# Cross-attention keys and queries: rounded weights meet both halves of x in one 512-column matmul

## The reference, cut to what matters

```
def memory_cross_attention(h, mem_n, w_q, w_kv, w_o):
    q = (h @ w_q).reshape(B, S, 4, 256)                    # "xq": queries
    kv = (mem_n @ w_kv).reshape(B, 256, 2, 4, 256)         # "K": keys, "V": values
    k, v = kv[:, :, 0], kv[:, :, 1]
    s = einsum('bthd,bmhd->bhtm', q, k) * 256 ** -0.5
    p = softmax(s, axis=-1)
    return einsum('bhtm,bmhd->bthd', p, v).reshape(B, S, 1024) @ w_o
```

## Time and profile before

| | us |
|---|---|
| median of 3 runs | 1287.78 (1287.45 to 1287.88) |
| the profiled execution's own time | 1287.96 |
| its span in the trace | 1286.2 |
| PE busy | 1273.2 (99%) |
| PEld busy | 1105.7 (86%) |
| DVE busy | 891.3 (69%) |
| ACT busy | 695.1 (54%) |
| DMA, mean share of its 16 engines for the weight queue | 51.6% |

### The profile page before, as it was taken

The page is one execution under the profiler, slowest core; times in us unless marked ns, Lnnn a source line. Parts: engine busy times, 40 slices in busy tenths (PEclk is TensorE's granted clock), DMA queues, the critical chain, the costliest instruction groups (busy, mean ns, idle before and its releaser), DMA issues.

```text
span 1286.2 us, 17766 instructions
## 1 busy us (share of the span) xinstructions
PE 1273.2 (99%) x7337; PEld 1105.7 (86%) x7337; DVE 891.3 (69%) x1053; ACT 695.1 (54%) x976; POOL 115.0 (9%) x176
## 2 busy tenths in 40 slices
PE   7999999999999999999999999999999999999999
PEld 7889898988888988889888888898887888888887
DVE  4657775776666776877676666767885566887775
ACT  5755554644444656565554444565565654655443
POOL 6200100100000100020100000101330003100000
PEclk9999999999999999999999999999999999999999
DMA  8754644556555543354455565563544445465552
GB/s 267 262 164 144 201 163 131 183 195 196 196 188 183 186 164 127 137 177 151 153 177 195 196 196 191 169 197 99 164 164 139 157 134 194 139 214 184 186 195 98
DMA packets 156113, 223.64 MB, mean 174 GB/s; under 512 B 6103, under 2 KB 107635, under 8 KB 156032
## 3 DMA queue, kind: packets, MB, share of 16 engines
q1 hardware_dynamic: 154528, 219.23, 51.6%
q0 software_dynamic: 1376, 3.22, 0.7%
q10 hardware_dynamic: 128, 0.05, 0.0%
HBM read 221.44 MB, written 1.05 MB: 173 GB/s over the span
## 4 chain that ended last, share of the span: by engine, by line
PE 90%; DVE 5%; ACT 2%; issue 1%; DMA 1%; POOL 0%; SPq 0%; ACTq 0%; DVEq 0%
PE ps L443 18%; PE ps L496 9%; PE ps L445 9%; PE ps L498 9%; PE ps L497 9%; PE ps L426 5%; PE ps L428 5%; PE ps L427 5%; PE ps L678 5%; PE ps L680 5%; PE ps L679 5%; DVE wlo L1803 2%; PE ps L517 1%; ACT whi L1221 1%; PE ps L461 1%
## 5 line engine op out<-in xcount | busy, mean ns | idle before, releaser
L1221 ACT ACTIVATE whi<-raw 128x1024 fp32r<-128x1024 f32 x411 | 424.5, 1052 | 313.8 <-PE ps L443 154.8
L1803 DVE TENSOR_TENSOR wlo<-raw,whi 128x1024 fp32r<-128x1024 f32 x408 | 490.1, 1232 | 140.4 <-ACT whi L1221 137.8
L443 PE MATMUL ps<-RR,whi 128*128 128x512 f32 x1024 | 353.9, 396 | 0.4 <-DVE wlo L1803 0.4
L445 PE MATMUL ps<-RR,wlo 128*128 128x256 f32 x1024 | 264.8, 279 | 0.1
L496 PE MATMUL ps<-whi,RR 128*128 128x512 f32 x592 | 236.7, 400 | 0.7 <-DVE wlo L1803 0.5
L498 PE MATMUL ps<-whi,RR 128*128 128x512 f32 x592 | 231.0, 390 | 0.0
L497 PE MATMUL ps<-wlo,RR 128*128 128x512 f32 x592 | 230.9, 390 | 0.0
L443 PEld LDWEIGHTS ps<-RR,whi 128*128 128x128 f32 x1024 | 184.9, 188 | 36.1 <-issue 0.7
L445 PEld LDWEIGHTS ps<-RR,wlo 128*128 128x128 f32 x1024 | 193.0, 188 | 11.9 <-DVE RR L1834 0.4
L426 PE MATMUL ps<-RR,whi 128*128 128x256 f32 x512 | 147.1, 287 | 0.9 <-DVE RR L1834 0.8
L428 PE MATMUL ps<-RR,wlo 128*128 128x256 f32 x512 | 144.8, 283 | 0.0
(11 more groups left out here) (357 smaller groups left out, 1311.9 us busy)
## 6 DMA issues: line engine op xcount, KB each, us to landing
raw<-in_ffn_w_gate_up SPq DMA_DIRECT2D x44, 1024.0 KB, 5.1
raw<-in_ffn_w_down SPq DMA_DIRECT2D x33, 1024.0 KB, 4.9
raw<-in_w_in SPq DMA_DIRECT2D x28, 1024.0 KB, 5.0
raw<-in_ffn_w_up SPq DMA_DIRECT2D x22, 1024.0 KB, 5.1
raw<-in_xa_w_kv SPq DMA_DIRECT2D x16, 1024.0 KB, 5.2
raw<-in_sb_w_qkv SPq DMA_DIRECT2D x12, 1024.0 KB, 5.1
raw<-in_ml_w_in SPq DMA_DIRECT2D x11, 1024.0 KB, 6.9
raw<-in_xa_w_q SPq DMA_DIRECT2D x8, 1024.0 KB, 5.2
```

The source lines that it names most:

```text
L443: m = pe.matmul(two(ps[:, bank, :]), p.hi[:, k, :], XT2[:, k, :, :], start=k == 0, stop=k == 7)
L445: pe.matmul(ps[:, bank, 0:256], p.lo[:, k, :], X.h[:, k, :], start=False, stop=False)
L1221: act.activation(p.hi, p.raw, ACT.Copy).then_inc(S["w_hi"], 2 if p.n == pool_piece.n + 1 else 1)
L1803: dve.tensor_tensor(p.lo, p.raw, p.hi.bitcast(F32), ALU.subtract).then_inc(S["w_lo"], 2 if p.n in (2, late_piece.n + 1) else 1)
```

## The change

For K0_0 to K0_3, K1_0 to K1_2 and all eight query chunks, `fm_piece` gives way to a new function `fm_wide`: eight matmuls of whi with hi and lo of x side by side (512 columns), then eight of wlo with hi of x (256 columns). The piece waits for `w_hi` before the first eight and for `w_lo` only before the second eight. Each piece now fills a whole bank, so a chunk takes two banks, and both halves of each must be added. ACT still copies only the first half of the banks (the rounded copy now rounds the first half). DVE does two instructions where it did one: lo = first half - hi, then, after the end of that, lo = lo + second half. For K0_1, whose banks are 0 and 3, both steps are done bank by bank, in four instructions of 256 columns. The banks are dealt out anew, with two new waits of TensorE on `K_dve` (before K0_2 and before K1_2), and its wait for `ml_og` 4 now stands ahead of K0_1. K1_3 stays narrow.

```diff
+            def fm_wide(name, X, banks, i):
+
+                p, o = C[name].pieces[i], ps[:, banks[i], :]
+                pe.wait_ge(S["w_hi"], p.n + 1)
+                for k in range(8):
+                    if X.met <= k:
+                        pe.wait_ge(X.sem, X.need[k])
+                        X.met = k + 1
+                    pe.matmul(two(o), p.hi[:, k, :], X.both[:, k, :, :], start=k == 0, stop=False)
+                pe.wait_ge(S["w_lo"], p.n + 1)
+                for k in range(8):
+                    m = pe.matmul(o[:, 0:256], p.lo[:, k, :], X.h[:, k, :], start=False, stop=k == 7)
+                m.then_inc(S["w_used"], 1)
...
             def keys(l, j, bank, M):
-                fm(f"K{l}_{j}", M, bank)
+                for i in range(2):
+                    fm_wide(f"K{l}_{j}", M, bank, i)
...
-            keys(0, 0, 1, M)
+            keys(0, 0, (1, 2), M)
...
-            keys(0, 1, 2, M)
             pe.wait_ge(S["ml_og"], 4)
-            keys(0, 2, 3, M)
+            keys(0, 1, (0, 3), M)
+            pe.wait_ge(S["K_dve"], 1)
+            keys(0, 2, (1, 2), M)
...
-            keys(1, 0, 4, M)
-            keys(1, 1, 5, M)
+            keys(1, 0, (6, 7), M)
+            keys(1, 1, (4, 5), M)
             X = norm_rows(2)
-            keys(1, 2, 6, M)
+            pe.wait_ge(S["K_dve"], 5)
+            keys(1, 2, (6, 7), M)
             pe.wait_ge(S["K_dve"], 6)
             feed_forward(0, X)
...
             def keys_lo(l, j, bank):
...
-                dve.tensor_tensor(Kl[:, 2 * j:2 * j + 2, :], two(ps[:, bank, :]), Kr[:, 2 * j:2 * j + 2, :].bitcast(F32),
-                                  ALU.subtract).then_inc(S["K_dve"], 1)
...
+                if (l, j) == (0, 1):
+                    for i in range(2):
+                        n = step(dve.tensor_tensor(lo[:, i, :], ps[:, bank[i], 0:256], hi[:, i, :].bitcast(F32), ALU.subtract))
+                    dve.wait_ge(S["dve_step"], n)
+                    for i in range(2):
+                        m = dve.tensor_tensor(lo[:, i, :], ps[:, bank[i], 256:512], lo[:, i, :].bitcast(F32), ALU.add)
+                    m.then_inc(S["K_dve"], 1)
+                    return
+                dve.wait_ge(S["dve_step"], step(dve.tensor_tensor(lo, part_of(bank, 0), hi.bitcast(F32), ALU.subtract)))
+                dve.tensor_tensor(lo, part_of(bank, 1), lo.bitcast(F32), ALU.add).then_inc(S["K_dve"], 1)
...
-                    dve.tensor_tensor(ql[h % 3], two(ps[:, h, :]), qh[h % 3].bitcast(F32), ALU.subtract).then_inc(S["xq"], 1)
+                    hi, lo, b = qh[h % 3].bitcast(F32), ql[h % 3], query_banks(h)
+                    dve.wait_ge(S["dve_step"], step(dve.tensor_tensor(lo, part_of(b, 0), hi, ALU.subtract)))
+                    dve.tensor_tensor(lo, part_of(b, 1), lo.bitcast(F32), ALU.add).then_inc(S["xq"], 1)
```

More of the change, by code:

```diff
@@ L75, with __init__ @@
 class Rows:
-    def __init__(self, h, l, sem, need):
-        self.h, self.l, self.sem, self.need, self.met = h, l, sem, need, 0
+    def __init__(self, h, l, sem, need, both=None):
+        self.h, self.l, self.sem, self.need, self.met, self.both = h, l, sem, need, 0, both
 class Tiles:
@@ L147, in build_program @@
         XTh, XTl, memTh, memTl = rr(0, 8), rr(2048, 8), rr(4096, 8), rr(6144, 8)
+        memT2 = RR[:, 4096:8192].rearrange("p (a k t) -> p k a t", a=2, t=256)
         XT2 = RR[:, 0:4096].rearrange("p (a k t) -> p k a t", a=2, t=256)
@@ L395, in early, with part_of, query_banks @@
             return x.rearrange("p (b h l) -> p b h l", h=2, l=L)[:, :, 0, :]
+        def part_of(banks, part):
+            return ps[:, banks[0]:banks[0] + 2, 256 * part:256 * part + 256]
+        def query_banks(h):
+            return (2, 3) if h % 2 else (0, 1)
         def half_bank(k, banks):
@@ L524, in norm_rows @@
                 turn(xn, 8, "n_x", (2 * no + 1, 2 * no + 2), (0, 1, 2, 3), "n_T")
-                return Rows(XTh, XTl, S["n_lo"], [8 * no + k + 1 for k in range(8)])
+                return Rows(XTh, XTl, S["n_lo"], [8 * no + k + 1 for k in range(8)], XT2)
             def mem_rows(i, part):
@@ L619, in cross_attention @@
                 pe.wait_ge(X.sem, X.need[2])
-                fm(f"xq{l}_0", X, 0)
+                for i in range(2):
+                    fm_wide(f"xq{l}_0", X, query_banks(0), i)
                 if 0 in between:
                     between[0]()
-                fm(f"xq{l}_1", X, 1)
+                for i in range(2):
+                    fm_wide(f"xq{l}_1", X, query_banks(1), i)
                 head_scores(0)
@@ L626, in cross_attention @@
                     between[1]()
-                fm(f"xq{l}_2", X, 2)
+                for i in range(2):
+                    fm_wide(f"xq{l}_2", X, query_banks(2), i)
                 head_scores(1)
@@ L632, in cross_attention @@
                 weights(l, 0)
-                fm_piece(f"xq{l}_3", X, 3, 0)
+                fm_wide(f"xq{l}_3", X, query_banks(3), 0)
                 head_scores(2)
@@ L636, in cross_attention @@
                 head_outputs(0)
-                fm_piece(f"xq{l}_3", X, 3, 1)
+                fm_wide(f"xq{l}_3", X, query_banks(3), 1)
                 weights(l, 2)
@@ L767, in tensor_program @@
             tm("mlo1b", X, 4, 8, (3, 0))
-            M = Rows(memTh, memTl, S["m_lo"], [k + 1 for k in range(8)])
+            M = Rows(memTh, memTl, S["m_lo"], [k + 1 for k in range(8)], memT2)
             pe.wait_ge(S["m_lo"], 8)
@@ L792, in tensor_program @@
             out_chunk("mlw", 3, O)
-            keys(0, 3, 5, M)
+            keys(0, 3, (4, 5), M)
             pe.wait_ge(S["V_dve"], 2)
@@ L1277, in keys_hi @@
                 act.wait_ge(S["w_used"], end(f"K{l}_{j}"))
-                act.activation(Kr[:, 2 * j:2 * j + 2, :], two(ps[:, bank, :]), ACT.Copy).then_inc(S["K_act"], 1)
+                if (l, j) == (0, 1):
+                    for i in range(2):
+                        m = act.activation(Kr[:, 2 * j + i, :], ps[:, bank[i], 0:256], ACT.Copy)
+                    m.then_inc(S["K_act"], 1)
+                    return
+                src = part_of(bank, 0) if (l, j) != (1, 3) else two(ps[:, bank, :])
+                act.activation(Kr[:, 2 * j:2 * j + 2, :], src, ACT.Copy).then_inc(S["K_act"], 1)
             def values_hi(l, j):
@@ L1312, in rows_hi @@
                     act.wait_ge(S["w_used"], end(f"xq{l}_{h}"))
-                    act.activation(qh[h % 3], two(ps[:, h, :]), ACT.Copy).then_inc(S["xq_hi"], 1)
+                    act.activation(qh[h % 3], part_of(query_banks(h), 0), ACT.Copy).then_inc(S["xq_hi"], 1)
                 def weights_hi(h):
@@ L1450, in scalar_program @@
                     act.wait_ge(*at("levels", 1))
-                    keys_hi(0, 0, 1)
+                    keys_hi(0, 0, (1, 2))
             past("K0_1")
-            keys_hi(0, 1, 2)
+            keys_hi(0, 1, (0, 3))
             past("K0_2")
-            keys_hi(0, 2, 3)
+            keys_hi(0, 2, (1, 2))
             past("V0_0a")
@@ L1473, in scalar_program @@
             past("K0_3")
-            keys_hi(0, 3, 5)
+            keys_hi(0, 3, (4, 5))
             past("V0_1a")
@@ L1485, in scalar_program @@
             past("K1_0")
-            keys_hi(1, 0, 4)
+            keys_hi(1, 0, (6, 7))
             past("K1_1")
-            keys_hi(1, 1, 5)
+            keys_hi(1, 1, (4, 5))
             norm_hi(2, gain1(0, 4))
             past("K1_2")
-            keys_hi(1, 2, 6)
+            keys_hi(1, 2, (6, 7))
             feed_forward(0)
@@ L1872, in keys_lo @@
                 dve.wait_ge(S["K_act"], 4 * l + j + 1)
-                dve.tensor_tensor(Kl[:, 2 * j:2 * j + 2, :], two(ps[:, bank, :]), Kr[:, 2 * j:2 * j + 2, :].bitcast(F32),
-                                  ALU.subtract).then_inc(S["K_dve"], 1)
+                hi, lo = Kr[:, 2 * j:2 * j + 2, :], Kl[:, 2 * j:2 * j + 2, :]
+                if (l, j) == (1, 3):
+                    dve.tensor_tensor(lo, two(ps[:, bank, :]), hi.bitcast(F32), ALU.subtract).then_inc(S["K_dve"], 1)
+                    return
+                if (l, j) == (0, 1):
+                    for i in range(2):
+                        n = step(dve.tensor_tensor(lo[:, i, :], ps[:, bank[i], 0:256], hi[:, i, :].bitcast(F32), ALU.subtract))
+                    dve.wait_ge(S["dve_step"], n)
+                    for i in range(2):
+                        m = dve.tensor_tensor(lo[:, i, :], ps[:, bank[i], 256:512], lo[:, i, :].bitcast(F32), ALU.add)
+                    m.then_inc(S["K_dve"], 1)
+                    return
+                dve.wait_ge(S["dve_step"], step(dve.tensor_tensor(lo, part_of(bank, 0), hi.bitcast(F32), ALU.subtract)))
+                dve.tensor_tensor(lo, part_of(bank, 1), lo.bitcast(F32), ALU.add).then_inc(S["K_dve"], 1)
             def values_lo(l, j):
@@ L2057, in vector_program @@
                     past("K0_0")
-                    keys_lo(0, 0, 1)
-            keys_lo(0, 1, 2)
+                    keys_lo(0, 0, (1, 2))
```

(11 more changed lines are left out.)

## The result

| | before | changed |
|---|---|---|
| median, us | 1287.78 (7 runs, 1287.45 to 1287.89) | 1291.93 (7 runs, 1291.85 to 1292.08) |
| ratio to before | | 1.0029, 95% interval 1.0020 to 1.0038 |
| span in the trace, us | 1286.2 | 1290.1 |

What follows compares the result with a forecast made beforehand. PE's stream of starts plus any stalls was taken as the bound. Stalls of 6.55 us less a gain of 2.25 made 4.3 slower, from 1287.78 to 1292.1 us; the 8-in-10 range was 1287.5 to 1294.4.

Steps and rivals of the forecast that it cites:

- The gain: PE in 15 changed chunks: fewer matmuls, same columns, save 0.15 us a chunk, 2.25 in all; bounds 1.8 and 3.
- The price of the second instruction: DVE's rests: everything behind an added dependent instruction comes 0.72 us later, bounds 0.60 and 0.85; K0_1's four, 0.85 later.
- The price of a late semaphore: PE waiting for DVE: first matmul 0.05 us after DVE's end, the second 0.11 later than usual, 0.16 together.
- Place 1: V0_0a after K0_2: PE waits for the first weight rest, behind K0_0's and K0_1's later rests; stall 1.25 us.
- Place 2: First cross-attention, transposes of head 1: PE waits for scaled weights delayed by head 2's extra instruction; stall 0.70 us.
- Place 3: Second cross-attention, transposes of head 1: DVE's chain ends 1.83 us later, ACT's waits moving along; PE stalls 2.30 us.
- Place 4: Last four score matmuls of head 3: PE waits for the query rest, 0.44 us in each layer, 0.88 in both.
- Place 5: First feed-forward: PE waits for K1_1's rest, behind K1_0's and the norm's rests; stall 1.42 us.
- hidden delays: Rival, all places: DVE's delays stay hidden and the wide stream pays, 1284.8 or 1285.5 us; chance 0.07.
- no gain: Rival, PE's wide matmuls: PE gains nothing, 1293.7 to 1294.3 us; chance 0.11 together with starved weights.
- only part of the stalls comes: Rival, places 1 and 3: stalls smaller, ACT's waits perhaps being PE's doing; 1290.3 us, called no change; chance 0.20.
- The starved weights: Rival, weight rests at places 1 and 3: delays reach second pieces and DMAs, 1294.5 us; chance 0.11 together with no gain.

Runs made afterwards that it cites:

- e1: Changed kernel without DVE's second instruction (second halves of the banks computed but never added); 1286.12 us, ratio 0.9986.
- e5: Changed kernel with the first piece of query chunk 0 taking wide and narrow matmuls in alternation; 1292.06 us, ratio 1.0034.
- e2: Kernel before, narrow matmuls and old banks, with each changed rest except K1_3's written twice, the second after the first's end; 1292.79 us, ratio 1.0041.

## Why the prediction was right

- *The gain.* Forecast 0.15 a chunk, 2.25 in all. Measured 0.16 to 0.19 for a chunk; summed over the 15 chunks without their stalls about 2.5. The Trainium skill (TensorE: Matmul & The Clock Gate, section "Back-to-back issue gap") gives N / 2.4 + 2.5 ns as the gap of an isolated matmul and says itself that a stream differs from it. The fixed cost of 2.5 ns would have given 0.6; K0_3's 5.56 against 5.75 and e1's 1.8 us rule that out here.
- *The price of the second instruction.* Forecast 0.72, seen 0.71 and 0.72. The price of a late semaphore, 0.05 and 0.11 for the second matmul: seen 0.05 and 0.11 at the feed-forward, but 0.15 and 0.07 at V0_0a.
- *Place 1, V0_0a.* Forecast 1.25; 12.66 - 11.37 + 0.06 = 1.35. Of the 0.1 that it missed, 0.06 is the start after the weight rest.
- *Place 2, head 1 in the first layer.* Forecast 0.70; 0.60 in the scores and 0.05 in the transposes behind.
- *Place 3, the same in the second layer.* Forecast 2.30 at the transposes; there it was 1.6, because TensorE had lost 0.64 before, in xq1_0. Together 2.2. VectorE's chain was right to its end: from the start of the layer's queries the scaled weights came 1.82 later than before (598.89 - 570.59 against 595.22 - 568.74), forecast 1.83, and e5 shows that the sum of the two stalls is what it fixes. What I left out is what the wide order asks of x: all eight rests in 1.6 us. That was luck: it cost nothing only because a longer wait stood behind it; with the chain shortened, as in e1 (1286.12 and not about 1285.4), it is paid.
- *Place 4, head 3.* Forecast 0.44 twice; 0.43 and 0.44.
- *Place 5, the feed-forward.* Forecast 1.42; 7.02 - 5.67 = 1.35, and about 0.1 in the first matmuls behind.
- *The new bank waits.* Forecast free, the one before K1_2 by only 0.3. The changed kernel's own view has no wait there, and its K1_0 and K1_1 take 11.15, as in e1, where VectorE is early.
- *Sum.* Stalls 6.55 forecast, 6.5 to 6.6 found; gain 2.25 forecast, 2.5 found; 4.3 forecast, 4.15 measured. The 0.25 too little for the gain is the largest error of a term that stands in the sum.

Of the rivals, hidden delays are ruled out by e2, no gain by e1. That only part of the stalls comes is ruled out by their sizes: ScalarE did follow VectorE in the second layer, and places 1 and 3 came whole. The starved weights did not come: the view of waits shows one new wait for a rest of weights, that of V0_0a, and none for a DMA but the very first. What stays open: whether the second layer can have wide queries at no loss, with another split of the memory's rests between the engines; that was not tried.

## What to carry to other kernels

Merging matmuls keeps the columns and saves only what each costs beside them, here about 10 ns for a k that took 360 (2.5 us over 240); any work that this puts on another engine must fit into the slack in front of each wait, and not into that engine's mean idle share (31% here). So read, for each consumer, the end of its producer against its arrival; by the rows of before, the five places here had 0.8 us or less in hand, four of them 0.5 or less. The gain can be kept by moving the producer's new instruction behind what is asked for first, or by leaving the change out where the producer is busy: with the rests also in another order, 12 of 15 chunks took 1285.77 where all 15 took 1287.54. Moving alone gave no clear gain here.

## What the runs showed of the hardware that I had not expected

The first is a matter of order: eight wide matmuls in a row move the demand for x forward, and xq1_0 stalled by 0.64 us, in e1 too, where VectorE does no more than before. The width alone doesn't do it: with wide and narrow in alternation in the first piece (e5) the stall was gone. The second is VectorE's price for a wait: an instruction of 128x512 on PSUM lasts 0.69, the next starts 0.60 or 0.61 after it if it doesn't wait, and 0.71 or 0.72 after it if it waits for its end. The third is that the time from the end of a VectorE instruction to the matmul that waited for it is not one number: 0.05 at the feed-forward, 0.15 at V0_0a; why is open. And the view of waits hides part of each stall behind the modelled end of the matmul before: 0.2 us shown for a stall of 0.4 at head 3, 0.2 for 0.64 in xq1_0.
